# A norm's weights travel with the first piece of turned x, and the other columns are loaded later

## The chip, the cores and the metric

The kernel runs on one core of one Trainium2 chip. The metric is the device time of one execution in microseconds (us). Three executions of the kernel before gave 764.67, 764.77 and 764.8 us; the median is 764.77.

## What is computed

Three transformer-like layers over 256 tokens of width 1024, all in float32. The change touches only the first layer's input, so this is what has to be seen:

```python
def rms_norm(x, g):
    y = xf * lax.rsqrt(jnp.mean(xf * xf, axis=-1, keepdims=True) + EPS)
    return y * g

def even_layer(x, g_norm, w_in, b_f, w_out):
    z = rms_norm(x, g_norm) @ w_in          # 256 x 1024 by 1024 x 8208
    qa, ka, va, ga, fa, qb, kb, vb, gb = jnp.split(z, cuts, axis=-1)
    ...
    return x + y @ w_out
```

A second layer (retention), a third (state space model beside attention, then a gated feed-forward block) and several more norms follow. Each norm has its weights g.

## The kernel before

**Units.** All weight matrices are cut into 230 units of 128 partitions x 1024 floats (512 KB), which go through a ring of four staging buffers. For each unit SyncE issues the load (L478), ScalarE writes its high part `w_hi` (L709, a cast to a shorter float32 form), VectorE writes the low part `w_lo` = stage - `w_hi` (L1085), and TensorE multiplies three times: high by high, low activations by high weights, high activations by low weights (L1786, L1790, L1794, four matmuls each). SyncE issues the load of unit u only when the low part of unit u - 4 has been made. So a unit's stage buffer, its load and TensorE's order hang on one another.

**Activations.** x is held in HBM a second time, turned: `x_turned` has 128 partitions and for each the eight tiles of 256 tokens. It is loaded in four pieces of two tiles (256 KB each, L457), each piece ahead of the unit that first needs it. ScalarE multiplies each tile by the norm's weights and casts it (L777, high part), VectorE makes the low part from the same two (L1145). The factor 1/rms is applied later to results, so the weights g are all that is needed before the first product. They are eight columns (`COL_EVEN`, one per tile) of the tile `col`, 128 partitions x 84 floats, which also holds the columns of all the other norms and of the state space model. `col` is loaded by one DMA, the first thing on ScalarE's queue (L769); ScalarE (L772) and VectorE (L1147) wait for it before their first use.

**The start.** Order of SyncE's queue: x's piece 0, unit 0 in two halves (L475, L476), unit 1 in two halves, unit 2, x's piece 1, unit 3, and then each unit as its buffer comes free. Order of ScalarE: issue of `col`, a small copy (L771), wait for `col`, then x tile 0, first half of unit 0 (L701), x tile 1, second half of unit 0, both halves of unit 1, issue of the identity matrix (L785), unit 2, x tiles 2 and 3, units 3 and 4, squares of x (L790), unit 5, x tiles 4 and 5, and so on, all written out by hand. VectorE follows in the same order. The next users of `col` on VectorE are at L1168 and L1175. TensorE first does twenty matmuls on ones (L1894) that only keep it busy, then unit 0 (L1808 and L1812), unit 1, and from unit 2 on the plain form.

The lines of ScalarE's start:

```python
            act.dma_start(col[:], t["columns"]).then_inc(columns_in, 16)
            act.wait_ge(fills, 1)
            nc.scalar.activation(rstd_in_q[:], neg_half[:, 0:NB], ACT.Copy)
            act.wait_ge(columns_in, 16)
            ...
            for i in range(2):
                hi_of_x(i)
                hi_of_half(0, i)
            for i in range(2):
                hi_of_half(1, i)
            next_unit[0] = HALVED
            act.dma_start(ident[:], t["ident"]).then_inc(ident_in, 16)
            split_hi(3)
```

Of the kernel before, what the change touches and what calls it, by code (L numbers as in the profile page):

```python
# [20 lines left out]
F32 = mybir.dt.float32  # L21
F32R = mybir.dt.float32r
I32 = mybir.dt.int32
ACT = mybir.ActivationFunctionType
ALU = mybir.AluOpType

P = 128
S = 256
NB = S // P
D = 1024  # L30
KD = D // P
# [104 lines left out]
def build(nc, t):  # L136
# [10 lines left out]
    with ExitStack() as ctx:  # L147
# [7 lines left out]
        x = sb("x", [P, NB, D])  # L155
        act_t = sb("act_t", [P, 16, S], F32R)
# [28 lines left out]
        col = sb("col", [P, N_ROWS])  # L185
        COL_EVEN, COL_ODD, COL_MIX, COL_FFN = 0, KD, 2 * KD, 3 * KD
# [35 lines left out]
        def over(name, at, shape, dt=F32):  # L222

            return nc.alloc_sbuf_tensor_at(name, shape, dt, offset=work_from + 4 * at)
# [7 lines left out]
        b_in = [over("b_in_re", 10240, [P, ST, SSM_C]), over("b_in_im", 10496, [P, ST, SSM_C])]  # L232
        b_tmp = [over("b_tmp0", 10752, [P, ST, SSM_C]), over("b_tmp1", 11008, [P, ST, SSM_C])]
        pow_tmp_early = over("pow_tmp_early", 10240, [P, 2, 512])
        x_turned, x_square = over("x_turned", 0, [P, KD, S]), over("x_square", 2048, [P, KD // 2, 2, S])

        y_lo = over("y_lo", 0, [P, 16, S], F32R)

# [33 lines left out]
        x_in, ident_in, columns_in, late_in, masks_in, wf_in, b_in_landed, c_in_landed, tables_in, params_in = sem("x_in"), sem("ident_in"), sem("columns_in"), sem("late_in"), sem("masks_in"), sem("wf_in"), sem("b_in_landed"), sem("c_in_landed"), sem("tables_in"), sem("params_in")  # L272
        x_turned_in = [sem(f"x_turned_in_{i}") for i in range(4)]
# [6 lines left out]
        turned, act_hi, act_lo = sem("turned"), sem("act_hi"), sem("act_lo")  # L280
# [79 lines left out]
        def wait_lower(eng, u):  # L360

            if u in lower_by_pool:
                eng.wait_ge(lo_ready_pool, lower_by_pool.index(u) + 1)
            else:
                eng.wait_ge(lo_ready, sum(i not in lower_by_pool for i in range(u + 1)))
# [57 lines left out]
        def unit_source(name, j):  # L423
            kind, c = name
            per = chunks[name][2]
            ks = slice(j * per, (j + 1) * per)
            if kind in even_at:
                return w_even[:, ks, even_at[kind] + c * 512:even_at[kind] + (c + 1) * 512]
            if kind in odd_at:
                return w_odd[:, ks, odd_at[kind] + c * 512:odd_at[kind] + (c + 1) * 512]  # L430
            if kind in in_at:
                return w_in[:, ks, in_at[kind]:in_at[kind] + UNIT // per]
            if kind == "ffn":
                at = (j % 2) * DFF + c * 256
                return w_gu[:, (j // 2) * 4:(j // 2 + 1) * 4, at:at + 256]
            if kind in ("mix_attn", "mix_ssm"):
                at = CT if kind == "mix_attn" else 0
                return w_mix[:, at + j * per:at + (j + 1) * per, c * 512:(c + 1) * 512]
            w = {"even_out": w_even_out, "odd_out": w_odd_out, "glu": w_glu, "down": w_down}[kind]
            return w[:, ks, c * 512:(c + 1) * 512]  # L440
# [9 lines left out]

        @block.sync
        def _(sp_eng):
            x_columns = t["x_turned"].rearrange("p (k n) -> p k n", k=KD)

            def load_turned(i):

                sp_eng.dma_start(x_turned[:, 2 * i:2 * i + 2, :], x_columns[:, 2 * i:2 * i + 2, :]).then_inc(x_turned_in[i], 16)  # L457

            for u, name, j in units_in_order:
                if name == TOGETHER[0]:  # L460
                    load_turned(j)
                if u == X_AT:
                    for b in range(NB):
                        sp_eng.dma_start(x[:, b, :], t["x"][b * P:(b + 1) * P, :]).then_inc(x_in, 16)
                if u == MASKS_AT:
                    sp_eng.dma_start(neg_bias[:, 0, :], t["neg_bias"][:, 0, :]).then_inc(masks_in, 16)
                if u == TABLES_AT:
                    sp_eng.dma_start(neg_bias[:, 1:3, :], t["neg_bias"][:, 1:3, :]).then_inc(later_masks_in, 16)
                    for dst, src in ((rot[:], t["rot"]), (steps[:], t["steps"]), (decay, t["decay"])):
                        sp_eng.dma_start(dst, src).then_inc(late_in, 16)  # L470
                if u >= RING:
                    wait_lower(sp_eng, u - RING)
                dst = stage[:, u % RING, :].rearrange("p (t n) -> p t n", t=chunks[name][2])
                if u < HALVED:
                    sp_eng.dma_start(dst[:, 0, :], unit_source(name, j)[:, 0, :]).then_inc(half_landed[u], 16)  # L475
                    sp_eng.dma_start(dst[:, 1, :], unit_source(name, j)[:, 1, :]).then_inc(landed[u], 16)  # L476
                else:
                    sp_eng.dma_start(dst, unit_source(name, j)).then_inc(landed[u % RING], 16)  # L478

            for b in range(NB):  # L480
                for c in range(2):
                    half = slice(c * 512, (c + 1) * 512)
                    sp_eng.wait_ge(h_ready, NB + 2 * b + c + 1)
                    sp_eng.dma_start(t["out"][b * P:(b + 1) * P, half], x[:, b, half]).then_inc(out_stored, 16)
            sp_eng.wait_ge(out_stored, 16 * 2 * NB)
# [208 lines left out]
        def _(act):  # L694
            next_unit = [0]

            def hi_of_half(u, i):

                half = slice(i * UNIT // 2, (i + 1) * UNIT // 2)
                act.wait_ge(half_landed[u] if i == 0 else landed[u], 16)  # L700
                nc.scalar.activation(w_hi[:, u, half], stage[:, u, half], ACT.Copy).then_inc(hi_half_ready if i == 0 else hi_ready, 1)  # L701

            def split_hi(until):

                for u in range(next_unit[0], min(until, n_units)):
                    act.wait_ge(landed[u % RING], 16 * (u // RING + 1))
                    if u >= RING:
                        act.wait_ge(unit_used, u - RING + 1)
                    nc.scalar.activation(w_hi[:, u % RING, :], stage[:, u % RING, :], ACT.Copy).then_inc(hi_ready, 1)  # L709
                next_unit[0] = max(next_unit[0], min(until, n_units))  # L710
# [55 lines left out]
                act.wait_ge(turned, i + 1)  # L766
                nc.scalar.activation(head_gates(i), bank(GATE_TURN_BANKS[i]).rearrange("p (k n) -> p k n", k=2), ACT.Copy).then_inc(gate_copied, 1)

            act.dma_start(col[:], t["columns"]).then_inc(columns_in, 16)  # L769
            act.wait_ge(fills, 1)  # L770
            nc.scalar.activation(rstd_in_q[:], neg_half[:, 0:NB], ACT.Copy)  # L771
            act.wait_ge(columns_in, 16)  # L772

            def hi_of_x(k):

                act.wait_ge(x_turned_in[k // 2], 16)
                nc.scalar.activation(act_t[:, k, :], x_turned[:, k, :], ACT.Copy, scale=col[:, COL_EVEN + k:COL_EVEN + k + 1]).then_inc(act_hi, 1)  # L777

            for i in range(2):
                hi_of_x(i)  # L780
                hi_of_half(0, i)
            for i in range(2):
                hi_of_half(1, i)
            next_unit[0] = HALVED
            act.dma_start(ident[:], t["ident"]).then_inc(ident_in, 16)  # L785
            split_hi(3)

            def square_of_turned(i):

                nc.scalar.activation(x_square[:, i], x_turned[:, 2 * i:2 * i + 2, :], ACT.Square).then_inc(x_squared, 1)  # L790

            hi_of_x(2)
            hi_of_x(3)
            split_hi(5)
            square_of_turned(0)
            square_of_turned(1)
# [151 lines left out]
            for b in range(NB):  # L948
                ins = nc.scalar.activation(qkv[:, b, 0:SINK_H, :], result(("sq", 0))[:, b, :].rearrange("p (h d) -> p h d", d=HD), ACT.Copy,
                                           scale=rstd_in_q[:, b:b + 1])  # L950
# [119 lines left out]
        def _(dve):  # L1070
# [8 lines left out]
            def split_lo(until):  # L1079

                for u in range(next_unit[0], min(until, n_units)):
                    if u in lower_by_pool:
                        continue
                    dve.wait_ge(hi_ready, u + 1)
                    nc.vector.tensor_tensor(w_lo[:, u % RING, :], stage[:, u % RING, :], w_hi[:, u % RING, :].bitcast(F32), ALU.subtract).then_inc(lo_ready, 1)  # L1085
                next_unit[0] = max(next_unit[0], min(until, n_units))
# [12 lines left out]
            TT, TS, STT = nc.vector.tensor_tensor, nc.vector.tensor_scalar, nc.vector.scalar_tensor_tensor  # L1099
# [42 lines left out]
            def lo_of_x(k):  # L1142

                dve.wait_ge(act_hi, k + 1)
                STT(act_t[:, KD + k, :], x_turned[:, k, :], col[:, COL_EVEN + k:COL_EVEN + k + 1], act_t[:, k, :].bitcast(F32), ALU.mult, ALU.subtract).then_inc(act_lo, 1)  # L1145

            dve.wait_ge(columns_in, 16)  # L1147
            for i in range(2):
                lo_of_x(i)
                lo_of_half(0, i)  # L1150
# [9 lines left out]

            lo_of_x(2)
            lo_of_x(3)
            split_lo(6)
            add_square(1)
            lo_of_x(4)
# [160 lines left out]
            for half in range(2):  # L1326
# [10 lines left out]
                for i in range(16 + 2):  # L1337
                    n = 16 * half + i
# [1044 lines left out]
```

## Time and profile before

| what | value |
|---|---|
| median of three executions | 764.77 us |
| the profiled execution, its own time | 764.88 us |
| its span in the trace | 763.1 us |
| TensorE (PE) busy | 752.2 us, 99% |
| VectorE (DVE) busy | 527.8 us, 69% |
| ScalarE (ACT) busy | 413.0 us, 54% |
| GpSimd (POOL) busy | 219.1 us, 29% |
| TensorE in the chain that ended last | 94% |

The profiled execution's time is 1.78 us longer than its span, for what lies around the traced instructions. Times in the rows below count from the span's start.

### The profile page before, as it was taken

What the parts mean: (1) busy time and instruction counts of PE and PEld (TensorE: products, weight loads), DVE (VectorE), ACT (ScalarE), POOL (GpSimd) and SP (SyncE); (2) the same over time, 40 slices, a digit from 0 to 9 for tenths busy, and PEclk for the clock granted to TensorE, in tenths of its full rate; (3) what the DMA queues carried; (4) which work ended last, traced back from release to release, by engine and by line L of the source; (5) the groups of instructions that cost most, each with busy time, mean ns of one, the idle gap of its engine ahead of it and who ended that gap; (6) DMA issues with size and microseconds to landing.
All of it is one profiled execution on the core that took longest, in us unless ns stands there. A gap on an engine that the chain in (4) does not pass through costs nothing.

```text
span 763.1 us, 12350 instructions
## 1 busy us (share of the span) xinstructions
PE 752.2 (99%) x4922; PEld 641.9 (84%) x4922; DVE 527.8 (69%) x786; ACT 413.0 (54%) x665; POOL 219.1 (29%) x175
## 2 busy tenths in 40 slices
PE   9999999999999999999999999999999999999997
PEld 7888887899777899887778888998878888888885
DVE  5876956765587558875567855788887677667553
ACT  6675468443586454453354554737857556455351
POOL 2113604794930000073029900126012011011010
PEclk9999999999999999999999999999999999999999
DMA  8989897578522746555444665430455656654741
GB/s 277 226 190 273 234 214 197 152 158 203 149 84 90 229 130 214 164 183 155 133 130 148 193 223 175 144 121 31 166 192 166 191 172 191 204 186 162 248 166 55
DMA packets 79065, 131.99 MB, mean 173 GB/s; under 512 B 4656, under 2 KB 28496, under 8 KB 79008
## 3 DMA queue, kind: packets, MB, share of 16 engines
q1 hardware_dynamic: 77072, 126.01, 56.0%
q0 software_dynamic: 1648, 5.09, 2.2%
q8 instruction: 39, 0.64, 0.3%
q14 instruction: 18, 0.15, 0.1%
q10 hardware_dynamic: 288, 0.11, 0.1%
HBM read 130.12 MB, written 1.06 MB: 172 GB/s over the span
## 4 chain that ended last, share of the span: by engine, by line
PE 94%; DVE 2%; ACT 2%; issue 1%; DMA 1%; DVEq 0%; ACTq 0%
PE ps L1786 15%; PE ps L1790 15%; PE ps L1794 15%; PE ps L1861 11%; PE ps L1843 7%; PE ps L1869 6%; PE ps L1848 4%; PE ps L1823 3%; PE ps L1827 3%; PE ps L1831 3%; PE ps L1939 2%; PE ps L2329 1%; PE ps L1972 1%; PE ps L2206 1%; PE ps L1957 1%; PE ps L2158 1%
## 5 line engine op out<-in xcount | busy, mean ns | idle before, releaser
L1085 DVE TENSOR_TENSOR w_lo<-stage,w_hi 128x1024 fp32r<-128x1024 f32 x224 | 292.4, 1330 | 140.6 <-ACT w_hi L709 139.8
L709 ACT ACTIVATE w_hi<-stage 128x1024 fp32r<-128x1024 f32 x230 | 239.1, 1061 | 216.4 <-PE ps L1794 98.8
L1786 PE MATMUL ps<-w_hi,act_t 128*128 128x512 f32 (+1 forms) x368 | 100.5, 396 | 0.2 <-ACT act_t L736 0.2
L1794 PE MATMUL ps<-w_lo,act_t 128*128 128x512 f32 (+1 forms) x368 | 96.5, 385 | 0.0
L1861 PE MATMUL ps<-act_t,w_hi 128*128 128x512 f32 x352 | 84.1, 391 | 0.0
L1794 PEld LDWEIGHTS ps<-w_lo,act_t 128*128 128x128 f32 x368 | 68.1, 188 | 14.0
L1790 PE MATMUL ps<-w_hi,act_t 128*128 128x512 f32 (+1 forms) x304 | 79.5, 384 | 0.0
L1786 PEld LDWEIGHTS ps<-w_hi,act_t 128*128 128x128 f32 x368 | 66.5, 188 | 15.4 <-issue 2.5
L1861 PEld LDWEIGHTS ps<-act_t,w_hi 128*128 128x128 f32 x352 | 64.7, 188 | 12.6
L1790 PEld LDWEIGHTS ps<-w_hi,act_t 128*128 128x128 f32 x304 | 56.1, 188 | 11.7
L1843 PE MATMUL ps<-act_t,w_hi 128*128 128x512 f32 x224 | 56.4, 394 | 0.0
L1843 PEld LDWEIGHTS ps<-act_t,w_hi 128*128 128x128 f32 x224 | 40.9, 192 | 6.9
L1869 PEld LDWEIGHTS ps<-act_t,w_lo 128*128 128x128 f32 x352 | 45.1, 191 | 1.6
L1869 PE MATMUL ps<-act_t,w_lo 128*128 128x256 f32 x352 | 45.7, 283 | 0.0
L682 POOL TENSOR_TENSOR big<-big 128x512 f32<-128x512 f32 x11 | 14.3, 1297 | 107.0 <-ACT big L1048 107.0
L1790 PE MATMUL ps<-w_hi,y_lo 128*128 128x512 f32 x128 | 34.2, 389 | 0.0
L1848 PEld LDWEIGHTS ps<-act_t,w_lo 128*128 128x128 f32 x224 | 30.7, 193 | 2.2
L1848 PE MATMUL ps<-act_t,w_lo 128*128 128x256 f32 x224 | 31.3, 282 | 0.0
L1790 PEld LDWEIGHTS ps<-w_hi,y_lo 128*128 128x128 f32 x128 | 24.0, 188 | 5.1
L1823 PE MATMUL ps<-act_t,w_hi 128*128 128x256 f32 x192 | 27.4, 285 | 0.0
L1827 PE MATMUL ps<-act_t,w_hi 128*128 128x256 f32 x192 | 26.9, 283 | 0.0
L1831 PE MATMUL ps<-act_t,w_lo 128*128 128x256 f32 x192 | 26.9, 283 | 0.0
(401 smaller groups left out, 1228.8 us busy)
## 6 DMA issues: line engine op xcount, KB each, us to landing
stage<-in_even_w_in SPq DMA_DIRECT2D x62, 512.0 KB, 5.4
stage<-in_odd_w_in SPq DMA_DIRECT2D x48, 512.0 KB, 4.4
stage<-in_w_gate_up SPq DMA_DIRECT2D x44, 512.0 KB, 4.6
stage<-in_w_down SPq DMA_DIRECT2D x22, 512.0 KB, 4.3
stage<-in_even_w_out SPq DMA_DIRECT2D x16, 512.0 KB, 4.3
stage<-in_odd_w_out SPq DMA_DIRECT2D x16, 512.0 KB, 4.3
stage<-in_w_in SPq DMA_DIRECT2D x10, 512.0 KB, 4.4
stage<-in_w_out SPq DMA_DIRECT2D x8, 512.0 KB, 4.2
```

The source lines that it names most:

```text
L709: nc.scalar.activation(w_hi[:, u % RING, :], stage[:, u % RING, :], ACT.Copy).then_inc(hi_ready, 1)
L1085: nc.vector.tensor_tensor(w_lo[:, u % RING, :], stage[:, u % RING, :], w_hi[:, u % RING, :].bitcast(F32), ALU.subtract).then_inc(lo_ready, 1)
L1786: mm(out[:, b, :], a_hi(k)[:, tok[b]], hi[:, i, :], start=(k == 0), stop=False)
L1790: mm(out[:, b, :], a_lo(k)[:, tok[b]], hi[:, i, :], start=False, stop=False)
L1794: ins = mm(out[:, b, :], a_hi(k)[:, tok[b]], lo[:, i, :], start=False, stop=(k == k_tiles - 1))
L1823: mm(out[m], columns(hi[:, i, :], m), act_t[:, k, :], start=(k == 0 and m % 2 == 0), stop=False, skip_group_check=True)
L1827: mm(out[m], columns(hi[:, i, :], m), act_t[:, KD + k, :], start=False, stop=False, skip_group_check=True)
L1831: ins = mm(out[m], columns(lo[:, i, :], m), act_t[:, k, :], start=False, stop=(k == k_tiles - 1), skip_group_check=True)
L1843: mm(bank(WIDE[name][m]).rearrange("p (v n) -> p v n", v=2), columns(hi[:, i, :], m), both[:, :, k, :], start=(k == 0), stop=False, skip_g ...
L1848: ins = mm(bank(WIDE[name][m], S), columns(lo[:, i, :], m), act_t[:, k, :], start=False, stop=(k == k_tiles - 1), skip_group_check=True)
L1861: mm(ffn_result(name[1], j % 2)[:, m, :, :], hi[:, i, w[m]], both[:, :, k, :], start=(k == 0), stop=(k == KD - 1), skip_group_check=True)
L1869: ins = mm(ffn_result(name[1], j % 2)[:, m, 0, :], lo[:, i, w[m]], act_t[:, k, :], start=False, stop=(k == KD - 1), skip_group_check=True)
```

## The change

The norm's eight weights per partition are put in front of the turned x, both in HBM (rows of 2,056 floats instead of 2,048) and in SBUF (one tile `gained_x`, of which `even_gain` and `x_turned` are views). The first piece becomes the weights and two tiles (2,080 bytes per partition instead of 2,048); the others keep their size. ScalarE and VectorE read the weights from there. `col` is no longer loaded at the start but on ScalarE's queue behind the casts of units 0 and 1, in front of the identity; ScalarE waits for it behind the casts of x tiles 2 and 3 and in front of those of units 3 and 4, VectorE at the corresponding place. `x_square` moves up by 128 floats. Nothing else changes.

```diff
@@ -232,7 +232,8 @@
-        x_turned, x_square = over("x_turned", 0, [P, KD, S]), over("x_square", 2048, [P, KD // 2, 2, S])
+        gained_x, x_square = over("gained_x", 0, [P, KD + KD * S]), over("x_square", 2176, [P, KD // 2, 2, S])
+        even_gain, x_turned = gained_x[:, 0:KD], gained_x[:, KD:KD + KD * S].rearrange("p (k n) -> p k n", k=KD)
@@ -450,11 +451,11 @@
-            x_columns = t["x_turned"].rearrange("p (k n) -> p k n", k=KD)
             def load_turned(i):
-                sp_eng.dma_start(x_turned[:, 2 * i:2 * i + 2, :], x_columns[:, 2 * i:2 * i + 2, :]).then_inc(x_turned_in[i], 16)
+                part = slice(KD + 2 * i * S if i else 0, KD + (2 * i + 2) * S)
+                sp_eng.dma_start(gained_x[:, part], t["x_turned"][:, part]).then_inc(x_turned_in[i], 16)
@@ -766,15 +767,13 @@
-            act.dma_start(col[:], t["columns"]).then_inc(columns_in, 16)
             act.wait_ge(fills, 1)
             nc.scalar.activation(rstd_in_q[:], neg_half[:, 0:NB], ACT.Copy)
-            act.wait_ge(columns_in, 16)
             def hi_of_x(k):
                 act.wait_ge(x_turned_in[k // 2], 16)
-                nc.scalar.activation(act_t[:, k, :], x_turned[:, k, :], ACT.Copy, scale=col[:, COL_EVEN + k:COL_EVEN + k + 1]).then_inc(act_hi, 1)
+                nc.scalar.activation(act_t[:, k, :], x_turned[:, k, :], ACT.Copy, scale=even_gain[:, k:k + 1]).then_inc(act_hi, 1)
@@ -782,6 +781,7 @@
             next_unit[0] = HALVED
+            act.dma_start(col[:], t["columns"]).then_inc(columns_in, 16)
             act.dma_start(ident[:], t["ident"]).then_inc(ident_in, 16)
             split_hi(3)
@@ -791,6 +791,7 @@
             hi_of_x(2)
             hi_of_x(3)
+            act.wait_ge(columns_in, 16)
             split_hi(5)
@@ -1142,9 +1143,8 @@
-                STT(act_t[:, KD + k, :], x_turned[:, k, :], col[:, COL_EVEN + k:COL_EVEN + k + 1], act_t[:, k, :].bitcast(F32), ALU.mult, ALU.subtract).then_inc(act_lo, 1)
-
-            dve.wait_ge(columns_in, 16)
+                STT(act_t[:, KD + k, :], x_turned[:, k, :], even_gain[:, k:k + 1], act_t[:, k, :].bitcast(F32), ALU.mult, ALU.subtract).then_inc(act_lo, 1)
@@ -1160,6 +1160,7 @@
             lo_of_x(2)
             lo_of_x(3)
+            dve.wait_ge(columns_in, 16)
             split_lo(6)
@@ -2369,7 +2370,8 @@
-    given["x_turned"] = _np.ascontiguousarray(given["x"].T.reshape(KD, P, S).transpose(1, 0, 2)).reshape(P, KD * S)
+    x_turned = given["x"].T.reshape(KD, P, S).transpose(1, 0, 2).reshape(P, KD * S)
+    given["x_turned"] = _np.ascontiguousarray(_np.concatenate([given["even_norm"].reshape(KD, P).T, x_turned], 1))
```

## Rows read from the trace of the kernel before

**Rows 1.** The page: the span, and the engines' shares of the chain that ended last
```profile
span 763.1 us, 12350 instructions
...
PE 94%; DVE 2%; ACT 2%; issue 1%; DMA 1%; DVEq 0%; ACTq 0%
```

**Rows 2.** Chain of waits, 0 to 40 us: start, length in us, what
```profile
0.74 3.94 DMA col<-in_columns
...
14.37 0.91 PE ps L1786 x4
...
25.25 0.91 PE ps L1786 x4
```

**Rows 3.** Timeline, DMA-issuing queues of SyncE and ScalarE: start, length, queue, line
```profile
0.73 0.37 SPq L457 DMA_DIRECT2D x_turned<-in_x_turned  x1
0.74 0.40 ACTq L769 DMA_DIRECT2D col<-in_columns  x1
...
1.15 0.42 SPq L475 DMA_DIRECT2D stage<-in_even_w_in  x1
...
8.09 0.34 ACTq L785 DMA_DIRECT2D ident<-in_ident  x1
...
13.78 0.37 SPq L478 DMA_DIRECT2D stage<-in_even_w_in  x1
```

**Rows 4.** DMA issues of 0.7 to 1.2 us: KB, us to landing
```profile
x_turned<-in_x_turned SPq DMA_DIRECT2D x1, 256.0 KB, 3.8
stage<-in_even_w_in SPq DMA_DIRECT2D x1, 256.0 KB, 4.0
col<-in_columns ACTq DMA_DIRECT2D x1, 42.0 KB, 3.9
```

**Rows 5.** Timeline, ScalarE; in brackets the idle time before and its releaser
```profile
4.70 0.51 ACT L777 ACTIVATE act_t<-x_turned,col 128x256 fp32r<-128x256 f32 x1 [2.03 <-DMA col<-in_columns]
5.20 0.63 ACT L701 ACTIVATE w_hi<-stage 128x512 fp32r<-128x512 f32 x1
...
8.08 0.64 ACT L701 ACTIVATE w_hi<-stage 128x512 fp32r<-128x512 f32 x1 [0.65 <-DMA stage<-in_even_w_in]
9.41 1.06 ACT L709 ACTIVATE w_hi<-stage 128x1024 fp32r<-128x1024 f32 x1 [0.69 <-DMA stage<-in_even_w_in]
...
11.43 1.06 ACT L709 ACTIVATE w_hi<-stage 128x1024 fp32r<-128x1024 f32 x1 [0.16 <-DMA stage<-in_even_w_in]
...
19.78 1.06 ACT L709 ACTIVATE w_hi<-stage 128x1024 fp32r<-128x1024 f32 x1 [0.39 <-DMA stage<-in_even_w_in]
```

**Rows 6.** Timeline, TensorE's weight loads: units 0 and 3
```profile
5.88 0.77 PEld L1808 LDWEIGHTS ps<-w_hi,act_t 128*128 128x128 f32 x4 [0.45 <-ACT w_hi L701]
...
13.99 0.87 PEld L1786 LDWEIGHTS ps<-w_hi,act_t 128*128 128x128 f32 x4
```

**Rows 7.** DMA issues: unit 3 (at 4.03), identity (8.09), positions, unit 7 (13.78)
```profile
stage<-in_even_w_in SPq DMA_DIRECT2D x1, 512.0 KB, 7.4
...
ident<-in_ident ACTq DMA_DIRECT2D x1, 64.0 KB, 5.1
...
pos_i<-in_positions POOLq DMA_DIRECT2D x2, 0.5 KB, 5.7
...
stage<-in_even_w_in SPq DMA_DIRECT2D x1, 512.0 KB, 6.0
```

**Rows 8.** DMA queues, 2 to 4, 8.1 to 11, 11 to 13 us: packets, MB, share
```profile
q1 hardware_dynamic: 261, 0.49, 89.9%
q10 hardware_dynamic: 138, 0.04, 10.3%
...
q1 hardware_dynamic: 594, 1.13, 105.5%
q10 hardware_dynamic: 2, 0.00, 0.1%
...
q10 hardware_dynamic: 142, 0.06, 11.1%
```

## The prediction

> **What bounds the kernel now.** I read the page first: the span is 763.1 us, and 94% of the chain that ended last is TensorE [rows 1]. So a change pays if it lets TensorE's real work start earlier, and costs what it makes TensorE wait later. Then the chain of waits over the first 40 us, which shows what TensorE's start hangs on: the columns' DMA for 3.94 us from 0.74, then two ScalarE casts, then matmuls without a gap [rows 2]. A unit takes TensorE 2.72 us (three passes of 0.91): unit 3 begins at 14.37 and unit 7 at 25.25 [rows 2]. Whatever moves TensorE's first weight load at 5.88 [rows 6], or opens a gap behind it, moves the end one for one; I found no wait of TensorE's on work that would not shift along with it.
>
> The queue's timeline gives the issues: x's first piece at 0.73, the columns at 0.74, unit 0's first half at 1.15 [rows 3]. The view of DMA issues gives the landings: 3.8, 3.9 and 4.0 us later, that is 4.53, 4.68 (by the chain's 3.94) and 5.15 [rows 4]. What the reader should see is how close the three are. ScalarE's timeline fits: it starts casting x at 4.70, 0.02 behind the columns, and the half unit at 5.20 without idling [rows 5]. TensorE's first weight load follows 0.05 behind the end of that cast (5.83).
>
> **The start: the columns no longer gate it.** With the weights in x's first piece ScalarE can cast x at 4.53 + 0.02 = 4.55 and is done at 5.06. But the half unit lands at 5.15, so its cast starts at 5.17 and not at 5.20: of the 0.15 us between x and the columns only 0.03 is to be had, since the half unit is late next. More comes only if the DMAs themselves land earlier, by r, because 42 KB are gone from ahead of them. Between 2 and 4 us the columns' queue (q10) used 10.3% of 16 engines, so 0.21 us of all of them [rows 8]; I take r = 0.2 (0.17 net, after 4 KB more in x's piece). Bounds: r = 0 if the longer x rows break into more packets and so cost what the columns did; r = 0.74 if the columns are to blame for all that the loads lack there against later: 0.49 MB in 2 us against 1.13 MB in 2.9, or 0.78 in 2, and 0.29 MB at 390 GB/s is 0.74 us [rows 8]. So the start gains 0.03 to 0.77, and I take 0.2. TensorE's warm-up does not stand in the way: its weight loads had been idle for 0.45 us at 5.88 [rows 6].
>
> x's rows in HBM are now 8,224 bytes apart, where they were 8,192. The first layer's unit rows are at such an uneven distance already (8,208 floats, 32,832 bytes), and SyncE's queue, units for the most part, moved 1.13 MB in the 2.9 us from 8.1 to 11, 390 GB/s [rows 8]; so I charge nothing for it. By the Trainium skill (DMA: Bandwidth & Descriptors, How a descriptor splits into AXI transactions) a descriptor that does not start at a multiple of 256 B fetches bytes it does not use; on a row of 64 beats that would be some 3 or 4 more, an estimate of 5 to 7%. On a piece that is followed by its neighbour in 0.62 us (4.53 to 5.15) that rule would take 0.04 us from the 0.2; the net cost below would be the same, and the first rival's time 764.61 in place of 764.57.
>
> VectorE's wait goes too, at no gain: it waits for ScalarE's first cast anyway. The ScalarE issue of 0.40 at 0.74 [rows 3] lay beside an idle engine, so removing it gives nothing.
>
> **The columns moved behind the first two units.** ScalarE's queue now issues them just behind its last half cast, where the identity was issued at 8.09 [rows 3], and the identity 0.4 us later. The issue cost itself, 0.40 more, is hidden: the next cast, unit 2, begins at 9.41 and idled 0.69 for its own load [rows 5]. The identity's first reader (L1104) stands far behind, after the first ten units, so it has all the time.
>
> What is not hidden is the new wait. It stands behind the cast of x's tile 3 and in front of the cast of unit 3, which ran at 11.43 after 0.16 idle [rows 5]. Behind it on ScalarE are the casts of units 3, 4 and 5, the squares and every later cast; VectorE waits for each to make the low part; SyncE's queue waits for VectorE's low part of unit 3 before it issues unit 7; TensorE waits for unit 3. So: when do the columns land? The identity, issued in that very slot on that queue, took 5.1 us [rows 7], and its packets did not move for three of them: 2 until 11.0, 142 from 11 to 13 [rows 8]. A small load issued there stands behind the units that are on their way. The columns have as many packets, so I take 5.1: 8.09 + 5.1 = 13.19; up to 0.2 earlier if the stream is ahead by r; I take 13.1. Bounds: 3.9 us, what the columns took at 0.74, gives 12.0; 7.4 us, unit 3's load, the longest issued in the first 16 us [rows 7], gives 15.5.
>
> Unit 3's cast then starts at 13.12 instead of 11.43, ends at 14.18 (1.06 each [rows 5]), and TensorE's weight load can follow 0.05 later, at 14.23. Now it stands at 13.99 [rows 6]. So TensorE comes to unit 3 at 13.79 if the start gained 0.2, waits 0.44 and leaves 0.24 later than now. In general the change costs max(-gain at the start, landing + 1.13 - 13.99): the full 0.2 is kept only if the columns land by 12.66, and nothing is lost up to 12.86.
>
> Further down the delay finds cover. VectorE's low part of unit 3 (1.23 us) is done at 15.4, and TensorE wants it 1.8 us behind 14.23. Unit 7's load, issued at 13.78 as soon as that low part was done [rows 3], would go at 15.4 and land 6.0 us later [rows 7], at 21.4; its cast then ends at 22.5 instead of 20.84 (19.78 + 1.06 [rows 5]), and TensorE wants it at 25.25 [rows 2]: 2.7 us to spare. Units 4 and 5 gain on TensorE, since a cast takes 1.06 and a unit 2.72. If this cover were gone (less than 1.7 us ahead at unit 7) the same delay would be paid once more; it is not.
>
> **The sum.** Start -0.2, new wait +0.44, net +0.24. The profiled execution took 764.88 us, 1.78 beside its span of 763.1; it stands 0.11 over the median of 764.77. Against its own time the sum is 765.12, against the median **765.0**.
>
> **Rivals.** *The columns arrive in time, and the start's gain is kept.* They must land by 12.66, so within 4.6 us of an issue at 8.09; time -0.2, 764.57, or down to 764.0 with the upper bound of r. For it: at 0.74 they took 3.9, and 42 KB are less than the identity's 64. Against it: the identity in the same slot, and the two position loads of half a KB, 5.7 us in the middle [rows 7]: size does not set it. By the Trainium skill (DMA: Bandwidth & Descriptors, Queues, rings and completion order) each DMA engine goes round between the queues that have work, so a short load on ScalarE's queue would not stand behind SyncE's backlog; that rule, this rival's, would give about 764.55. The trace speaks against it: 2 packets in 2.9 us while the other queue moved 594 [rows 8]. Chance 0.28.
>
> *The change removes a wait that another takes at once.* x's piece and the half unit land as before (r = 0), the columns land between 12.7 and 12.9: within 0.1 of nothing, 764.8. The landings 0.15 and 0.47 us around the columns' speak for it. Chance 0.10.
>
> *The columns stand behind whole units and stop TensorE.* The place is the same wait before unit 3. It passes 0.2% (1.53 us, about what a measurement of this kernel can tell from no change) if they land at 14.39 or later, 6.3 us after the issue. At unit 3's 7.4 us they land at 15.5, and the cost is 15.5 + 1.13 - 13.99 = 2.6 us: 767.4. For it: loads of SyncE's queue issued from 4 us on do take 6 to 7.4. Against: these have 512 KB, and the small loads of this stretch took 5.1 to 5.7 [rows 7]. Chance 0.05.
>
> The forecast itself, a net cost of 0.1 to 1.2 us by the columns' late landing, has 0.55; 0.02 is left for something that gains over 1.53 us, which nothing in the rows offers, as the half unit's landing stands in the way.
>
> **The numbers.** The likeliest case gives 765.0. The range goes down to 764.3, which holds the kept gain at its likely size and half of its upper bound, and up to 766.0, a landing 6.0 us after the issue. Faster by over 0.2%: 0.02. Slower by over 0.2%: 0.05. Within: 0.93.
>
> **What would show it.** Right: ScalarE's first cast of x starts before 4.6 and the half unit's cast is released by its own load; its cast of unit 3 starts near 13.1 and is released by the columns' DMA; TensorE has one gap of some 0.4 us before unit 3, at about 14; SyncE issues unit 7 near 15.4; nothing waits behind that. A cast of unit 3 before 12.8 and no gap makes the first rival right. A first cast of the half unit later than 5.2 would show x's longer rows to cost what the columns did. The prediction is wrong if the time leaves 764.3 to 766.0, or if a second gap opens near unit 7.

## The result, and the profile after

Fourteen executions of each kernel gave a median of 766.48 us (765.68 to 767.23) against 765.04 us (764.42 to 765.93): a ratio of 1.0018, with a 95% interval of 1.0011 to 1.0025. The change costs 1.4 us, with 0.8 to 1.9 inside the interval. The forecast was 765.0, a cost of 0.24 over the 764.77 then known, with a range up to 766.0. Its sign and its place were right and its size was not. The kernel before itself came out 0.27 us higher than its first three executions had it.

The profiled execution took 766.54 us with a span of 764.7. The page of the kernel after answers to [rows 1]:

```profile
span 764.7 us, 12350 instructions
...
PE 88%; DVE 4%; DMA 3%; ACT 2%; issue 1%; SPq 0%; DVEq 0%; ACTq 0%
```

TensorE's share of the chain falls from 94 to 88%, and DMA's rises from 1 to 3%. The chain's first 20 us show where, and answer to [rows 2]; columns as there:

```profile
2.56 6.51 DMA stage<-in_even_w_in
...
9.10 4.92 DMA col<-in_columns
...
14.04 1.07 ACT w_hi L710
...
15.15 1.20 PE ps L1787 x4
...
26.35 0.91 PE ps L1787 x4
```

Two DMAs now stand in the chain, one behind the other: the second half of unit 1 (landing 9.07), which releases ScalarE's last half cast and so the issue of the columns, and the columns themselves (landing 14.02). The timeline of ScalarE in the kernel after answers to [rows 5]:

```profile
3.65 0.51 ACT L776 ACTIVATE act_t<-gained_x 128x256 fp32r<-128x256 f32 x1 [1.44 <-DMA gained_x<-in_x_turned]
4.40 0.63 ACT L702 ACTIVATE w_hi<-stage 128x512 fp32r<-128x512 f32 x1 [0.24 <-DMA stage<-in_even_w_in]
...
8.35 1.38 ACT L702 ACTIVATE w_hi<-stage 128x512 fp32r<-128x512 f32 x2 [2.29 <-DMA stage<-in_even_w_in]
9.10 0.38 ACTq L784 DMA_DIRECT2D col<-in_columns  x1
...
14.04 2.01 ACT L710 ACTIVATE w_hi<-stage 128x1024 fp32r<-128x1024 f32 x2 [1.77 <-DMA col<-in_columns]
...
22.39 1.06 ACT L710 ACTIVATE w_hi<-stage 128x1024 fp32r<-128x1024 f32 x1 [2.60 <-DMA stage<-in_even_w_in]
```

The first cast of x is a whole microsecond earlier than before (3.65 for 4.70), and the half unit's cast 0.80 earlier. Then ScalarE idles 2.29 us for unit 1, where before its casts of units 0 and 1 had one gap of 0.65 us, and 1.77 us for the columns in front of unit 3. TensorE's weight loads, in the same kernel, answer to [rows 6]:

```profile
5.15 0.76 PEld L1809 LDWEIGHTS ps<-w_hi,act_t 128*128 128x128 f32 x4
...
9.03 1.69 PEld L1809 LDWEIGHTS ps<-w_hi,act_t 128*128 128x128 f32 x8 [1.24 <-ACT w_hi L702]
...
11.68 0.87 PEld L1787 LDWEIGHTS ps<-w_hi,act_t 128*128 128x128 f32 x4
...
15.15 0.76 PEld L1787 LDWEIGHTS ps<-w_hi,act_t 128*128 128x128 f32 x4 [0.79 <-ACT w_hi L710]
```

TensorE starts 0.73 us earlier, waits 1.24 in front of unit 1 (for its first half, which took 6.2 us from its issue at 2.09 where before it took 4.7), comes to unit 2 at 11.68 (0.41 later than before) and to unit 3 at 15.15 (1.16 later). The DMA issues of the kernel after answer to [rows 4] and [rows 7]; the third row is unit 1's second half, issued at 2.56, which had taken 5.5 us before:

```profile
gained_x<-in_x_turned SPq DMA_DIRECT2D x1, 260.0 KB, 2.9
...
stage<-in_even_w_in SPq DMA_DIRECT2D x1, 256.0 KB, 3.2
...
stage<-in_even_w_in SPq DMA_DIRECT2D x1, 256.0 KB, 6.5
...
col<-in_columns ACTq DMA_DIRECT2D x1, 42.0 KB, 4.9
```

So the first two loads land 0.9 and 0.8 us sooner after their issue, the fourth lands 1.5 later and the fifth 1.0 later. How fast the loads went, by stretch; last column GB/s, in front of it the share of the DMA engines that was busy. First the kernel before:

```profile
2.00:4.00 2.00, 2.00 (x11) 2.00 (x11) 0.00 (x0) 0.66 (x2) 0.00 (x0) 1.00 1.00 264
4.00:7.00 3.00, 2.84 (x14) 2.30 (x13) 1.62 (x4) 2.27 (x5) 0.00 (x0) 1.00 0.97 266
```

Then the kernel after:

```profile
2.00:4.00 2.00, 2.00 (x11) 2.00 (x11) 0.00 (x0) 0.55 (x3) 0.00 (x0) 1.00 0.94 296
4.00:7.00 3.00, 3.00 (x17) 2.58 (x16) 2.21 (x4) 1.82 (x4) 0.00 (x0) 1.00 1.01 201
7.00:9.00 2.00, 1.23 (x6) 0.66 (x4) 0.00 (x0) 0.63 (x1) 0.00 (x0) 1.00 1.03 370
```

It moves more up to 4 us and much less from 4 to 7, with its engines busy all the while, so single packets take longer there. That stretch is unit 1's. Was it made by the change, and by which part of it?

### The profile page after: what moved, and what is told of

The parts are those of the page before. It is cut to its first block, busy times and chain, and to the rows that moved or that the text cites. A ratio compares the mean times of both kernels' runs of the same rounds, so it can differ in the third digit from the quotient of the medians.

```text
span 764.7 us, 12350 instructions
## 1 busy us (share of the span) xinstructions
PE 752.7 (98%) x4922; PEld 641.5 (84%) x4922; DVE 527.9 (69%) x786; ACT 411.9 (54%) x665; POOL 218.7 (29%) x175
## 4 chain that ended last, share of the span: by engine, by line
PE 88%; DVE 4%; DMA 3%; ACT 2%; issue 1%; SPq 0%; DVEq 0%; ACTq 0%
PE ps L1787 15%; PE ps L1791 15%; PE ps L1795 15%; PE ps L1862 11%; PE ps L1870 6%; PE ps L1844 4%; PE ps L1824 3%; PE ps L1832 3%; PE ps L1828 3%; DMA stage<-in_even_w_in 3%; PE ps L1849 2%; PE ps L1940 2%; DVE w_lo L1086 1%; PE ps L2330 1%; PE ps L1973 1%; PE ps L2207 1%
## 5 line engine op out<-in xcount | busy, mean ns | idle before, releaser
L1849 PEld LDWEIGHTS ps<-act_t,w_lo 128*128 128x128 f32 x224 | 30.7, 193 | 2.7 <-DVE w_lo L1086 0.5
L1849 PE MATMUL ps<-act_t,w_lo 128*128 128x256 f32 x224 | 31.4, 283 | 0.1
```

The costliest lines, as they stand in the source:

```text
L1849: ins = mm(bank(WIDE[name][m], S), columns(lo[:, i, :], m), act_t[:, k, :], start=False, stop=(k == k_tiles - 1), skip_group_check=True)
```

## The experiments

Fifteen runs followed: eleven new kernels, and four repeats. All but one were timed against the kernel before on the same chip, in 11 or 12 executions. A single interval is about 0.0009 wide on either side, 0.7 us, so below it is the traces and groups of medians that carry the argument as much as any one ratio. The ratio is not the quotient of the medians, and a few long executions move it. In the expectations a look is the trace of one execution.

Four theories. **W**: the wait before unit 3 costs. **A**: the columns' rows in front held the other loads back to a good pace; without them unit 1 is late. **B**: x's new rows make unit 1 late. **C**: unit 1 is late in most executions of any of these kernels, and the trace of before was a lucky one.

**The columns first again.** The changed kernel with the load back in front, without its early wait:

```diff
+            act.dma_start(col[:], t["columns"]).then_inc(columns_in, 16)
             act.wait_ge(fills, 1)
...
-            act.dma_start(col[:], t["columns"]).then_inc(columns_in, 16)
             act.dma_start(ident[:], t["ident"]).then_inc(ident_in, 16)
```

> The changed kernel, but the columns' load is issued first on ScalarE's queue again, as in the kernel before; nothing waits for it before unit 3. Theory A (with the columns' rows gone from the front, SyncE's loads run ahead and then unit 1's halves land 1.0 us later: 9.07 for 8.06): with the columns back in front unit 1's second half lands near 8.1 again, TensorE has no gap before units 1 and 3, and the time is that of the kernel before or up to 0.2 us less (ratio 0.9995 to 1.0003). Theory B (x's rows, now 8,224 bytes apart, make the loads late): unit 1 still lands near 9, TensorE has its gap of about 1 us before unit 1, and the ratio is 1.0005 to 1.0015.

Measured 765.37 against 765.10 us, 1.0004 (0.9996 to 1.0013), between the ranges of the two theories. Unit 1's second half took 6.6 us, not 5.5, and TensorE waited 1.11 us for unit 1. A falls: the columns in front do not bring unit 1 back. The larger part of the cost is gone all the same, and nothing waits before unit 3. TensorE's weight loads of units 2 and 3:

```profile
11.68 0.87 PEld L1787 LDWEIGHTS ps<-w_hi,act_t 128*128 128x128 f32 x4
...
14.40 0.87 PEld L1787 LDWEIGHTS ps<-w_hi,act_t 128*128 128x128 f32 x4
```

Unit 2 stands where it stood in the trace of the change, at 11.68, and unit 3 at 14.40 instead of 15.15. So of that trace's delay of 1.16 us at unit 3, the wait is 0.75 and the late loads of the start are 0.41.

**Late waits.** The changed kernel with both waits moved down to the first readers:

```diff
             hi_of_x(3)
-            act.wait_ge(columns_in, 16)
             split_hi(5)
...
+            act.wait_ge(columns_in, 16)
             for half, kind in enumerate(("ga", "gb")):
...
-            dve.wait_ge(columns_in, 16)
             split_lo(6)
...
             split_lo(7)
+            dve.wait_ge(columns_in, 16)
             TT(col[:, COL_MIX:COL_MIX + KD], col[:, COL_MIX:COL_MIX + KD], col[:, COL_FINAL:COL_FINAL + KD], ALU.mult).then_inc(col_ready, 1)
```

> The changed kernel with the two waits for the columns moved down to before their first readers (VectorE before L1168's product, ScalarE before the first gates); the load stays where the change put it. If the wait before unit 3 is what costs (0.75 of the 1.1 us by which TensorE is late at unit 3 in the changed kernel), the cast of unit 3 starts as its load lands, near 12.4, TensorE enters unit 3 some 0.4 us later than in the kernel before and the ratio is about 1.0006 to 1.0010. If the loads' lateness alone sets it, the gap before unit 3 stays and the ratio stays at 1.0015 to 1.0020.

765.85 against 765.10 us, 1.0009 (1.0001 to 1.0018): 0.69 us less than the change's 1.44. In this trace unit 1's second half took 7.1 us, so the cast of unit 3 stood at 13.04 and its weight load at 15.07, as late as in the trace of the change; but here it was the loads alone. W holds by the time; the trace is of an execution with later loads. This was the first sign that traces of the same start differ by more than the effect under test.

**The layout alone**, in the kernel before, and **aligned rows**, in the changed one:

```diff
-                 nc.scalar.activation(act_t[:, k, :], x_turned[:, k, :], ACT.Copy, scale=even_gain[:, k:k + 1]).then_inc(act_hi, 1)
+                 nc.scalar.activation(act_t[:, k, :], x_turned[:, k, :], ACT.Copy, scale=col[:, COL_EVEN + k:COL_EVEN + k + 1]).then_inc(act_hi, 1)
...
-        even_gain, x_turned = gained_x[:, 0:KD], gained_x[:, KD:KD + KD * S].rearrange("p (k n) -> p k n", k=KD)
+        even_gain, x_turned = gained_x[:, 64 - KD:64], gained_x[:, 64:64 + KD * S].rearrange("p (k n) -> p k n", k=KD)
```

(The first pair is of the layout run, which also has the columns' load and waits where they were; the second of the aligned one.)

> The kernel before, with only the new layout of x in HBM and SBUF (the weights travel with it and aren't used from there; the columns are loaded first and waited for as before). Theory B (the rows 8,224 bytes apart make the loads late): unit 1's second half lands after 8.5 and the ratio is 1.0008 or more. Theory A (the missing columns' load lets the stream run ahead): the ratio is 0.9997 to 1.0004 and unit 1's second half lands near 8.1.

> The changed kernel with x's rows padded to 64 + 2048 floats, the eight weights in the last of the 64, so that x itself and the pieces 1 to 3 start at multiples of 256 bytes in HBM; the first piece has 2,080 bytes per partition as in the change. Theory B: unit 1's loads come back to 8.1, the ratio falls to 1.0003 or less. Theory A: unit 1's second half lands near 9 and the ratio stays at 1.0011 to 1.0025.

The layout alone: 765.88 against 765.10, 1.0015 (1.0006 to 1.0023), unit 1's second half 7.1 us. Two of its twelve executions took 767.67 and 768.36; the medians alone give 1.0010. Aligned rows, 8,448 bytes apart: 766.47 against 765.10, 1.0019 (1.0010 to 1.0027), unit 1's second half 7.0, both gaps there as in the change (1.35 and 1.02 us). Alignment does not bring anything back: B in the form that odd addresses slow the loads falls. What is left of B is that the rows are no longer 8,192 bytes apart.

**The kernel before, traced twice more.** No edit.

> The kernel before, unchanged, timed and looked at again. The first four variants, the one with nothing but the new layout among them, all show unit 1's halves landing 1 to 2 us late, and only the one trace of the kernel before does not. Theory C (unit 1 is late in most executions of any of these kernels, and that trace was a lucky one): this look has unit 1's second half after 8.5 as well, and a gap of TensorE before unit 1. Theory B (the layout makes it late): this look has it near 8.1 and no gap, as the first. Either way the ratio is 1.0, within 0.0005: it measures how far the comparison can be trusted.

> The kernel before, unchanged, a third look. As for the second: theory C has unit 1's second half after 8.5 here too, theory B near 8.1.

765.30 against 765.15, 1.0006 (0.9995 to 1.0017), so a ratio of 1.0006 is what no change can give. One execution of 769.38 us makes most of it; the medians alone give 1.0002. In the second trace (765.87 us) unit 1's second half lands at 8.4, just ahead of the 8.5 that C named, and TensorE has no gap before unit 1. It comes to unit 3 at 14.46 all the same, 0.47 later than in the first trace, and not because of a load. The first eight weight loads of unit 0 take 2.25 us:

```profile
5.82 2.25 PEld L1808 LDWEIGHTS ps<-w_hi,act_t 128*128 128x128 f32 x8 [0.40 <-ACT w_hi L701]
```

In the first trace they take 1.7 us, 188 ns each; here single ones take up to 333 ns. Three more traces have the same, and no gap before unit 1 either: the SBUF shift (2.39 us), x before unit 1 (2.47) and the layout alone, again (2.56). The granted clock reads 1.00 in all of them, and why TensorE is slow there was not found.

The third trace (one execution, 765.78 us) shows, for x's first piece and for unit 1's second half:

```profile
x_turned<-in_x_turned SPq DMA_DIRECT2D x1, 256.0 KB, 3.3
...
stage<-in_even_w_in SPq DMA_DIRECT2D x1, 256.0 KB, 6.9
```

and TensorE in it waits for unit 1 twice:

```profile
9.21 0.76 PEld L1808 LDWEIGHTS ps<-w_hi,act_t 128*128 128x128 f32 x4 [0.93 <-ACT w_hi L701]
10.21 0.77 PEld L1808 LDWEIGHTS ps<-w_hi,act_t 128*128 128x128 f32 x4 [0.24 <-ACT w_hi L701]
```

The same kernel, the same queue, and the fifth load takes 5.5, 5.8 and 6.9 us in three traces. C holds in part: the first trace had the best of them, in its loads and on TensorE, but only one of the other two passes the 8.5 us of theory C.

**The layout in two halves.** Eight unused floats behind each HBM row; and x shifted by 32 bytes in SBUF only:

```diff
+    given["x_turned"] = _np.ascontiguousarray(_np.concatenate([x_turned, given["even_norm"].reshape(KD, P).T], 1))
...
+        x_turned, x_square = over("x_turned", KD, [P, KD, S]), over("x_square", 2176, [P, KD // 2, 2, S])
```

> The kernel before with eight unused floats behind each row of turned x in HBM: rows 8,224 bytes apart, nothing else. Theory B in its HBM form (the distance of the rows sets how the loads of the start go): x's first piece lands near 3.6 in place of 4.5, unit 1's second half after 8.5, the ratio is 1.0008 or more. If the layout has no part in it: as the kernel before, ratio 1.0 within 0.0005.

> The kernel before with turned x 32 bytes further up in SBUF and its squares moved up as in the change; HBM as before. Theory B in its SBUF form (destinations shifted by 32 bytes slow the writes or ScalarE's and VectorE's reads): the ratio is 1.0008 or more. If the layout has no part in it or its HBM side alone: ratio 1.0 within 0.0005.

The row distance: 765.58 against 765.15, 1.0006 (0.9997 to 1.0015). The SBUF shift: 765.20 against 765.15, 1.0001 (0.9992 to 1.0010). The shift in SBUF is cleared as far as 0.0010 can show; the row distance, expected at 1.0008 or more, is left in doubt by its own ratio.

**The change without the layout**, with both positions of the waits. The weights come by a load of their own:

```diff
-            act.dma_start(col[:], t["columns"]).then_inc(columns_in, 16)
+            act.dma_start(even_gain[:], t["even_gain"]).then_inc(gain_in, 16)
...
-            act.wait_ge(columns_in, 16)
+            act.wait_ge(gain_in, 16)
...
+            act.dma_start(col[:], t["columns"]).then_inc(columns_in, 16)
             act.dma_start(ident[:], t["ident"]).then_inc(ident_in, 16)
```

> The change with turned x left as it was in HBM and SBUF (rows 8,192 bytes apart): the eight weights come by a load of their own, 4 KB, first on ScalarE's queue, and the columns are moved and waited for as in the change. Theory W (the wait before unit 3 is the larger part, about 0.65 us, and the new layout the rest): ratio 1.0005 to 1.0012, below the change's. Theory S (the loads of the start run ahead of themselves without the columns in front, and the layout has no part): ratio 1.0013 to 1.0022, as the change. Either way ScalarE's cast of unit 3 is released by the columns near 14.

> The kernel of the run before with both waits for the columns moved down to their first readers, as in the run with the late waits. Theory W: no cost is left, the ratio is 0.9995 to 1.0004, 0.0006 to 0.001 below the run before. Theory S: ratio 1.0006 to 1.0012, as the late waits gave with the new layout. No cast waits for the columns.

With the waits as in the change 765.59 against 765.37, 1.0002 (0.9994 to 1.0011), which is below what either theory gave; with late waits 765.08 against the same 765.37, 0.9995 (0.9986 to 1.0004), as W said. The pair differs in the waits alone, by 0.51 us, and all eleven executions with the wait (765.28 us and more) lie above the median without. Neither kernel has the change's early start: the 4 KB of weights took 4.0 and 3.9 us, as long as the 42 KB of columns had, and ScalarE's first cast stands at 4.75 and 4.64. The trace of the first shows the cast of unit 3 and the weight load that waits for it:

```profile
13.97 2.01 ACT L711 ACTIVATE w_hi<-stage 128x1024 fp32r<-128x1024 f32 x2 [1.63 <-DMA col<-in_columns]
```

```profile
15.08 0.76 PEld L1791 LDWEIGHTS ps<-w_hi,act_t 128*128 128x128 f32 x4 [0.77 <-ACT w_hi L711]
```

In the trace of the second both stand near where they did in the kernel before:

```profile
11.90 1.07 ACT L711 ACTIVATE w_hi<-stage 128x1024 fp32r<-128x1024 f32 x1
```

```profile
13.97 0.87 PEld L1791 LDWEIGHTS ps<-w_hi,act_t 128*128 128x128 f32 x4
```

That second kernel has the lowest ratio of all. Its interval takes in 1, so it is not shown to beat the kernel before.

**Both repeated.** The layout alone and the change, on another chip, no edit.

> The layout alone in the kernel before, a second time on another chip, since its first ratio of 1.0015 (1.0006 to 1.0023) stands against 1.0006 (0.9997 to 1.0015) for the row distance alone. If the layout costs, the ratio is 1.0005 or more again; if the first was chance, it is 1.0003 or less.

> The changed kernel, unchanged, a second look and a second timing. Unit 1's second half lands between 8.8 and 9.8 (theory C: it did in all looks but two of the kernel before), the columns land 4.9 us behind their issue, near 14 or later, and TensorE has two gaps, about 1 us before unit 1 and about 0.8 before unit 3. Ratio 1.0011 to 1.0025.

The layout alone: 765.75 against 765.37, 1.0006 (0.9997 to 1.0015). The change: 766.33 against 765.37, 1.0012 (1.0003 to 1.0021), with waits of 1.91 us before unit 1 and 0.67 before unit 3, the columns landing at 14.45. On this same chip the change stands 0.74 us above the old layout with the same waits.

**The slow stretch.** All three start from the kernel with the old layout and late waits. The first loads x's second piece before unit 1:

```diff
-                if name == TOGETHER[0]:
+                if name == TOGETHER[0] and j != 1:
                     load_turned(j)
+                if u == 1:
+                    load_turned(1)
```

The second loads unit 1 whole (`if u < HALVED and u != 1:`), and the third adds eight unused floats behind each row of x in HBM, as above.

> The kernel with the old layout and late waits, but SyncE loads x's second piece before unit 1 instead of behind unit 2. If the slow stretch of the loads (some 150 to 250 GB/s between 4.5 and 7 us, where 400 follow) belongs to the time, whatever is on its way then, the x piece falls into it, lands near 8 and unit 1 behind it near 9.5, and the ratio is 1.0003 to 1.0012. If it belongs to unit 1's addresses, the x piece lands within 0.8 us of unit 0's second half, near 6.5, and unit 1 is 1 to 2 us behind that.

> The same kernel with unit 1 loaded by one DMA of 512 KB instead of two of 256 KB; ScalarE's first half cast of it waits for the whole. If the number of loads that are open at once makes the slow stretch, unit 1 lands by 8.1 and the ratio falls to 0.9992 or less; if not, it lands between 8.5 and 9.5 as in the other looks and the ratio is 0.9995 to 1.0008.

> The same kernel (old layout, late waits, weights by their own load) with nothing changed but eight unused floats behind each row of turned x in HBM, so rows 8,224 bytes apart. If the row distance is what costs, x's first piece lands 2.8 to 3.3 us after its issue (3.7 without), unit 1's second half 6.5 or more after its own (5.9 without), and the ratio is 0.0004 to 0.0010 above that of the kernel without, so 0.9999 to 1.0005. If the distance has no part in it, the ratio is 0.9995 within 0.0003.

The piece of x in unit 1's place, issued at 2.10, took 4.7 us and landed at 6.8; unit 1's halves landed at 8.1 and 9.1 behind it; 765.50 against 765.28, 1.0004 (0.9994 to 1.0013). The landing lies nearer to what was expected if the stretch belongs to unit 1, but 6.8 is no prompt landing either; the loads moved 256, 250 and 254 GB/s in the three microseconds from 5 to 8, and the ratio is inside the other theory's range, so it is not settled. Unit 1 whole: it landed at 8.6, 765.72 against 765.28, 1.0006 (0.9997 to 1.0015), with 188 GB/s from 5 to 7 us; one open load less does not make the stretch fast. Wide rows: 765.90 against 765.28, 1.0007 (0.9998 to 1.0015), unit 1's second half 7.0 us where the kernel without them had 5.9. The ratio is above both ranges named for it, and x's first piece took 3.4 us, not 3.3 or less; and the kernel without them, at 0.9995, was timed on another chip. In the kernel with wide rows the stretch looks like this:

```profile
5.00:6.00 1.00, 1.00 (x6) 0.87 (x6) 0.97 (x2) 1.00 (x3) 0.00 (x0) 1.00 0.85 156
6.00:7.00 1.00, 1.00 (x6) 0.73 (x5) 1.00 (x3) 0.39 (x1) 0.00 (x0) 1.00 0.85 154
```

and in the one without:

```profile
5.00:6.00 1.00, 0.80 (x5) 0.61 (x5) 0.69 (x2) 1.00 (x3) 0.00 (x0) 1.00 0.96 209
6.00:7.00 1.00, 1.00 (x5) 0.75 (x5) 1.00 (x3) 0.69 (x2) 0.00 (x0) 1.00 0.86 168
```

**All traces together.** Us from issue to landing of x's first piece and of unit 1's second half, the start of unit 3's first weight load, and the median less that of the kernel before on its chip (no value for unit 1 where it was loaded in another way):

| kernel | rows of x, bytes | x's piece | unit 1's 2nd half | unit 3 | median, us over before |
|---|---|---|---|---|---|
| before | 8,192 | 3.8 | 5.5 | 13.99 | |
| before, 2nd trace | 8,192 | 3.7 | 5.8 | 14.46 | +0.15 |
| before, 3rd trace | 8,192 | 3.3 | 6.9 | 14.65 | |
| SBUF shift | 8,192 | 3.3 | 6.3 | 14.27 | +0.05 |
| old layout, late waits | 8,192 | 3.7 | 5.9 | 13.97 | -0.29 |
| x before unit 1 | 8,192 | 3.4 | | 14.38 | +0.22 |
| unit 1 whole | 8,192 | 3.4 | | 14.73 | +0.44 |
| layout alone | 8,224 | 3.1 | 7.1 | 15.10 | +0.78 |
| layout alone, again | 8,224 | 3.3 | 6.2 | 14.33 | +0.38 |
| row distance alone | 8,224 | 3.1 | 6.6 | 14.31 | +0.43 |
| wide rows, late waits | 8,224 | 3.4 | 7.0 | 14.74 | +0.62 |
| columns first | 8,224 | 2.9 | 6.6 | 14.40 | +0.27 |
| late waits | 8,224 | 2.9 | 7.1 | 15.07 | +0.75 |
| **change** | 8,224 | 2.9 | 6.5 | 15.15 | +1.44 |
| **change**, again | 8,224 | 2.9 | 7.0 | 15.59 | +0.96 |
| aligned rows | 8,448 | 2.8 | 7.0 | 15.72 | +1.37 |
| old layout, the change's waits | 8,192 | 3.8 | 6.5 | 15.08 | +0.22 |

The time of the traced execution less the start of unit 3's weight load is 750.8 to 751.4 us in sixteen of the seventeen traces, and 752.0 in that of the SBUF shift. So what is lost by unit 3 is, within some 0.6 us, what is lost at the end.

Three readings. The four traces at the bottom have the wait; in each of them the weight load of unit 3 starts 6.0 to 6.2 us behind unit 1's landing (9.09 and 15.08 in the last). In the others, where unit 1's second half took 6.2 us or more, it starts 5.2 to 5.6 behind. The wait costs 0.51 us on one chip (the pair of the old layout) and 0.62 on another (aligned rows less late waits, which differ in alignment too); the change less late waits gives 0.69 by the change's first timing and 0.21 by its second.

Second, the layout without the wait: the six medians of the wide rows, columns first and late waits among them, are 0.54 us over before on average, those of the five others 0.11, so about 0.4 us. Of the four timings with the layout or the row distance alone only one has an interval above 1, the one with the two long executions. The traces do not put all of this on the loads: the layout alone, again, comes to unit 3 0.34 late with no gap before unit 1, by its slow weight loads.

Third, unit 1's second half takes 5.5 to 6.9 us with the old rows (mean of six traces 6.15) and 6.2 to 7.1 with the wide ones (mean of the nine 6.8), though x's piece itself is faster with them. Within the wide rows, four traces with the columns in front have 6.2 to 7.1 and the four with nothing in front 6.5 to 7.1, so A has little left. That is the direction of B, with the two groups overlapping. But the old rows show the same trade by themselves: the two traces whose x piece took 3.3 us have 6.3 and 6.9 for unit 1, the four with 3.7 or 3.8 have 5.5 to 6.5. So an early first load and a late fifth go together in either layout, and it is open which makes which. I call the row distance the likely cause of that 0.4, and not shown.

## Why the prediction was wrong

**The new wait: mechanism, place and formula were right.** The forecast was that TensorE would come to unit 3 later by landing + 1.13 - 13.99. The columns landed at 14.02; 14.02 + 1.13 - 13.99 = 1.16, and TensorE came at 15.15, 1.16 later. The columns took 4.9 us from their issue in both traces of the change (4.5 to 5.0 in the nine traces of kernels that moved them), 5.1 was taken from the identity, and the bounds of 3.9 and 7.4 were never approached. The rival by which the columns arrive in time fell: they had to land by 12.66 and landed at 14.02. Its mechanism fell less clearly than the forecast had it: in this trace ScalarE's queue, columns and identity together, moved 29 packets from 10 to 11 us and 108 from 11 to 12, beside 209 and 153 of SyncE's, so it was not held back until the other queue was empty.

**The step that failed is the issue time of the columns, "8.09 + 5.1 = 13.19; up to 0.2 earlier if the stream is ahead by r".** The issue stands behind the cast of unit 1's second half, and so behind that load's landing, which I took from one execution (8.06) and allowed to move in one direction only. It came at 9.07, and the issue at 9.10: 1.01 us late, less 0.2 for the shorter way to landing, which makes a landing of 14.02 out of 13.19 (13.1 taken) and a delay at unit 3 of 1.16 out of 0.24. The runs show why one trace could not give this term. It was an early draw: the same kernel has 8.4 and 9.5 in its other traces. And nine of nine traces with wide rows land it at 8.8 or later, as do three of the six with the old rows. Seen from there the term should have been a landing between 8.1 and 9.7, and with it a delay at unit 3 of 0.2 to 1.8 us, which reaches beyond the range's end of 1.2 over the median. I read a cost of tenths off a start whose fifth load scatters by more than a microsecond. Why that load scatters stays open.

**The start's gain was mis-sized too, and it did not matter.** TensorE's first weight load moved by 0.73 us, near the upper bound of 0.77 and not the 0.2 taken. But the step assumed that an earlier start is kept until unit 3. At unit 1 TensorE needs a load that is not earlier: it waited 1.24 us there and was 0.41 behind at unit 2. A gap before unit 1 was not in the forecast. The wait that I asked about, the half unit's, was the wrong one; the one that is late next was two loads further on.

**"So I charge nothing for it" of the row distance.** No cost of unaligned addresses shows (the aligned rows are as slow as the change), as the step said. But the rows' new distance is the likely source of some 0.4 us, not shown, and not through x's own piece, which became faster. The rule of the Trainium skill that was weighed there (DMA: Bandwidth & Descriptors, How a descriptor splits into AXI transactions) would have slowed x's piece, and the runs show no such thing: with the row distance alone changed it took 3.1 us, where the kernel before has 3.3 to 3.8, and in the change it took 2.9. Two small figures of the prediction do not come out there: 3 or 4 beats in 64 are 5 to 6%, and a gain of 0.2 gives 764.57, not 764.55.

**Cover further down: right.** Unit 7's load was issued at 16.46 and its cast ended at 23.45, with TensorE wanting it at 26.35: 2.9 us to spare where 2.7 were forecast. Both count to the matmuls; their weight loads stand 0.4 us earlier, at 25.96 and 24.87, so some 0.4 less was to spare in either. No second gap opened near it. The trace of the change has one of 0.5 us at L1849, which with the 1.16 at unit 3 makes up its 1.66 us over the first trace; the second trace of the kernel before has it too, the second trace of the change has not, so it is no part of the change.

Worked out again with what was measured, the change is the wait (0.2 to 0.7, 0.5 where one chip timed the pair) and what came with the layout (0.4 by the groups, 0.7 by the pair on one chip), 0.6 to 1.4 us; the two timings gave 1.44 and 0.96, each with some 0.6 either way. The start's gain is in neither, since TensorE waited for unit 1 behind it.

## What to carry to other kernels

A load moved from the head of a kernel to behind its first work inherits the scatter of everything in front of it: read the traces of several executions before a cost under a microsecond is taken from the first ten. When a wait is moved, put it in front of the first reader and not at the place where the load was expected; here that alone is worth about 0.5 us. And a start that comes earlier pays only as far as the next load does: name the load that is late next, and the one behind it.

## What the runs showed of the hardware that I had not expected

The same loads in the same order do not come at the same time. Unit 1's second half landed 5.5, 5.8 and 6.9 us after its issue in three traces of one kernel. All executions of the kernel before but one lie between 764.4 and 766.7 us; that one took 769.4.

In every trace the loads were slow in the same stretch: 131 to 258 GB/s from 5 to 7 us, after 266 to 359 from 3 to 4 and ahead of 361 or more from 8 to 10. The first trace of the kernel before had 258 and 238 there, the one of the change 178 and 188. One open load less did not help. Why it is slow there was not found.

The size of a short load hardly shows: at the head of ScalarE's queue 4 KB took 3.6 to 4.0 us in five traces and 42 KB took 3.1 to 3.9 in eight.

With the rows of x 8,224 or 8,448 bytes apart x's first piece landed 2.8 to 3.4 us after its issue, with 8,192 bytes 3.3 to 3.8, the kernel with the shift in SBUF alone (3.3) among these. The ranges overlap.
